# Gated recurrence of one layer: decayed keys and queries carried from level to level, gate units cut in quarters

## The reference, cut to what matters

```
f = lb + (1 - lb) * sigmoid(f_logit)
log_f = log(max(f, 1e-6)); key = 1 - f
state = 0
for t: state = exp(log_f[t])[:, None] * state + key[t][:, None] * v[t][None, :]
       out[t] = q[t] @ state
```

## Time and profile before

| | |
|---|---|
| median of 3 runs | 3363.87 us (3363.17 to 3366.28) |
| the profiled execution | 3358.75 us |
| its span | 3356.6 us |
| TensorE busy | 3220.8 us, 96% |
| VectorE busy | 1618.3 us, 48% |
| ScalarE busy | 1085.7 us, 32% |
| GpSimd busy | 322.1 us, 10% |
| granted TensorE clock, mean | 0.98 |

### The profile page before, as it was taken

One profiled execution on the slowest core, in us unless ns is written; L12 is line 12 of the kernel. 1 busy time (PEld: TensorE's weight loads), 2 busy tenths in 40 slices (PEclk: granted clock), 3 DMA queues, 4 the chain that ended last, 5 costly groups with the idle time before them and its releaser, 6 DMA issues.

```text
span 3356.6 us, 38850 instructions
## 1 busy us (share of the span) xinstructions
PE 3220.8 (96%) x15546; PEld 2652.5 (79%) x15546; DVE 1618.3 (48%) x1917; ACT 1085.7 (32%) x1157; POOL 322.1 (10%) x178
## 2 busy tenths in 40 slices
PE   6986899999999899999999999999999999999999
PEld 5865698888888789888888777888888777888887
DVE  5365454555334644555534755444433674454433
ACT  2223233444322333444423332233322332233232
POOL 1003110011000001001100200101100120011000
PEclk9998899999999999999999999999999999999999
DMA  3410131222332123122233212222232212222223
GB/s 138 127 46 30 38 144 45 88 99 88 113 126 76 51 74 128 38 98 90 100 112 91 81 63 88 88 101 93 95 106 103 77 63 88 88 88 100 100 100 113
DMA packets 47578, 299.94 MB, mean 89 GB/s; under 512 B 7075, under 2 KB 7331, under 8 KB 13012
## 3 DMA queue, kind: packets, MB, share of 16 engines
q1 hardware_dynamic: 42336, 288.01, 24.3%
q10 hardware_dynamic: 5108, 10.02, 1.3%
HBM read 293.26 MB, written 4.75 MB: 89 GB/s over the span
## 4 chain that ended last, share of the span: by engine, by line
PE 90%; DVE 5%; ACT 2%; issue 1%; POOL 1%; DMA 0%; another core or an unknown queue 0%; ACTq 0%; DVEq 0%; SPq 0%; POOLq 0%
PE G L409 80%; PE psS L869 1%; PE G L876 1%; PE psS L681 1%; DVE wL L1342 1%; PE psT L901 1%; PE psT L490 1%; ACT wH L982 1%; PE psS L465 1%; PE psS L768 1%; PE G L775 1%; DVE mxt L1532 1%; PE psS L462 0%; DMA x<-in_x 0%; DVE ws L1814 0%
## 5 line engine op out<-in xcount | busy, mean ns | idle before, releaser
L409 PE MATMUL G<-hH,wH 128*128 128x512 f32 x2624 | 1042.3, 397 | 11.0 <-DVE wL L1342 5.9
L409 PE MATMUL G<-hH,wL 128*128 128x512 f32 x2624 | 1027.5, 392 | 2.1 <-issue 2.1
L409 PE MATMUL G<-hL,wH 128*128 128x512 f32 x2624 | 1027.7, 392 | 0.0
L1342 DVE TENSOR_TENSOR wL<-raw,wH 128x2048 fp32r<-128x2048 f32 x266 | 647.7, 2435 | 673.3 <-ACT wH L982 673.0
L409 PE MATMUL G<-wsr,wH 128*128 128x512 f32 (+1 forms) x2400 | 713.9, 381 | 14.3 <-DVE ws L2031 9.7
L982 ACT ACTIVATE wH<-raw 128x2048 fp32r<-128x2048 f32 x266 | 506.8, 1905 | 456.0 <-PE G L409 441.5
L409 PEld LDWEIGHTS G<-hH,wH 128*128 128x128 f32 x2624 | 497.6, 190 | 121.0 <-issue 16.4
L409 PEld LDWEIGHTS G<-hH,wL 128*128 128x128 f32 x2624 | 496.3, 189 | 108.3 <-issue 2.5
L409 PEld LDWEIGHTS G<-hL,wH 128*128 128x128 f32 x2624 | 496.7, 189 | 103.4 <-issue 2.4
L409 PEld LDWEIGHTS G<-wsr,wH 128*128 128x128 f32 x2400 | 445.4, 190 | 101.3 <-DVE ws L2031 10.6
L409 PE MATMUL G<-wsr,wL 128*128 128x512 f32 (+1 forms) x1200 | 456.2, 380 | 0.0
(11 more groups left out here) (259 smaller groups left out, 2769.6 us busy)
## 6 DMA issues: line engine op xcount, KB each, us to landing
raw<-in_units SPq DMA_DIRECT2D x266, 1024.0 KB, 4.8
ws<-bias_rows SPq DMA_DIRECT2D x2, 1536.0 KB, 14.8
bias_rows<-ws ACTq DMA_DIRECT2D x1, 2560.0 KB
x<-in_x SPq DMA_DIRECT2D x4, 512.0 KB, 8.2
ws<-in_mem ACTq DMA_DIRECT2D x2, 1024.0 KB, 4.9
ws<-bias_rows ACTq DMA_DIRECT2D x1, 2048.0 KB, 8.4
out_x<-x SPq DMA_DIRECT2D x4, 512.0 KB, 7.6
ws<-in_decay ACTq DMA_DIRECT2D x1, 1280.0 KB, 13.0
```

Of the source, the lines that this page charges most:

```text
L409: mm = pe.matmul(o, mv if swap else wt, wt if swap else mv, start=first and n == 0, stop=last and n == 2)
L1342: V.tensor_tensor(wL[:, g.p, :], raw[:, g.p, :], wH[:, g.p, :].bitcast(F32), ALU.subtract)\
```

## The change

The running sum now starts anew in every block of 4 tokens (HG_BLOCK). ACT takes exp(cum) and exp(-cum) once, per head, and the exponential of each block's last sum, the decay of the whole block. DVE multiplies by q and key for level 0, and multiplies the key by its block's decay. POOL forms the decays of blocks of 8, 16, 32, 64 and 128 tokens by five small products of pairs, 128x256, 128x128, 128x64, 128x32 and 128x16 (`level_sums`, now line 2155). From level to level, DVE then multiplies in place (`grow`): keys of even blocks by the decay of the odd neighbour, queries of odd blocks by that of the even one, per head and behind that head's scores. `hz_ready` now counts heads. The banks of levels 6 and 7 are read by ACT (`hc_ready`). The two gate units are cut into quarters of 12 matmuls, one behind each level, unit one behind levels 0 to 3, unit two behind levels 4 to 7. The two steps that follow the gate units stand, on DVE, behind level 5 and behind level 6's products.

```
-HG_CHUNK = 64
+HG_BLOCK = 4
...
+        sums = {4: ws[:, RST, :].rearrange("p (h n) -> p h n", h=4)}
+        at = 0
+        for half in (8, 16, 32, 64, 128):
+            n = S // half
+            sums[half] = ws[:, SD + 2, at:at + 4 * n].rearrange("p (h n) -> p h n", h=4)
+            at += 4 * n
@@ -660,17 +667,18 @@
                     for lev in range(8):
-                        pe.wait_ge(hz_ready, lev + 1)
-                        zk = ZA if lev % 2 == 0 else ZB
-                        zq = ZB if lev == 0 else zk
                         for h in range(4):
                             n = lev * 4 + h
-
-                            wait(pe, hm_ready, n - 1)
-                            if lev == 0:
+                            pe.wait_ge(hz_ready, n + 1)
+
+                            if n >= 26:
+                                pe.wait_ge(hc_ready, n - 25)
+                            else:
+                                wait(pe, hm_ready, n - 1)
+                            if n == 0:
 
                                 pe.wait_ge(ms_ready, c.stat.v)
-                            k_, q_ = ws[:, zk + h, :], ws[:, zq + h, :]
+                            k_, q_ = ws[:, (ZB if lev == 0 else KEY) + h, :], ws[:, ZA + h, :]
                             if lev < 6:
                                 parts = [(ct * P, ct * P, ct * P, P) for ct in range(4)]
                             elif lev == 6:
@@ -682,9 +690,19 @@
                                                start=True, stop=True)
                             mm.then_inc(hs_done, 1)
 
-                        if lev in (1, 3):
-                            plain(h_op)
-                    pe.wait_ge(hm_ready, 32)
+                        q = lev % 4
+                        if q == 0:
+                            take_unit()
+                            take_job()
+                        for k in (2 * q, 2 * q + 1):
+                            for t in range(2):
+                                w0 = k * 256 + t * P
+                                mm = passes(G[:, c.job.p * 2 + t, :], w0, w0 + P, h_op, k, slice(0, S), k == 0, k == KT - 1)
+                        if q == 3:
+                            end_job(mm)
+                            c.unit.off += 1
+                    pe.wait_ge(hm_ready, 24)
+                    pe.wait_ge(hc_ready, 8)
@@ -1158,23 +1176,24 @@
-                    for lev in range(8):
-                        z = flat(ZA if lev % 2 == 0 else ZB, 4)
-                        act.wait_ge(he_in, lev + 1)
-                        if lev == 0:
-                            activation(flat(ZA, 4), flat(ZB, 4), ACT.Exp, scale=-1.0)
-                            activation(flat(ZB, 4), flat(ZB, 4), ACT.Exp).then_inc(he_exp, 1)
-                            step()
-                        elif 2 ** (lev + 1) < HG_CHUNK:
-                            activation(z, z, ACT.Exp).then_inc(he_exp, 1)
+                    act.wait_ge(scan_ready, 1)
+                    activation(ws[:, RST, :], flat(CUM, 4).rearrange("p (n l) -> p n l", l=4)[:, :, 3], ACT.Exp)\
+                        .then_inc(t4_ready, 1)
+                    act.wait_ge(tn_ready, c.nrm.v + 4)
+                    for h in range(4):
+                        activation(ws[:, ZA + h, :], ws[:, CUM + h, :], ACT.Exp)
+                        activation(ws[:, ZB + h, :], ws[:, CUM + h, :], ACT.Exp, scale=-1.0).then_inc(he_exp, 1)
+                    step()
+                    step(store(ws[:, GG:GG + 2, :], ACT.Silu))
+                    for n in range(24, 32):
+                        act.wait_ge(hs_done, n + 1)
+                        b, h = psS[:, n % 2, :], n % 4
+                        if n < 28:
+                            ins = activation(hsx1[:, h], b.rearrange("p (k q) -> p k q", q=P)[:, 0:2, :], ACT.Copy)
                         else:
-
-                            half = 2 ** (lev + 1)
-                            z0, z1 = blocks(z, half)
-                            activation(z0, z0, ACT.Exp)
-                            activation(z1, blocks(flat(CUM, 4), half)[1], ACT.Exp).then_inc(he_exp, 1)
-                        if lev in (3, 5):
-                            step(store(ws[:, GG + lev - 3:GG + lev - 1, :], ACT.Silu))
+                            ins = activation(ws[:, SX2 + h, :], b, ACT.Copy)
+                        ins.then_inc(hc_ready, 1)
+                    step(store(ws[:, GG + 2:GG + 4, :], ACT.Silu))
@@ -1735,45 +1754,55 @@
-                    gq, key = flat(GQ, 4), flat(KEY, 4)
-
-                    def mask(lev):
+
+                    for h in range(4):
+                        dve.wait_ge(he_exp, h + 1)
+                        V.tensor_tensor(ws[:, ZA + h, :], ws[:, ZA + h, :], ws[:, GQ + h, :], ALU.mult)
+                        V.tensor_tensor(ws[:, ZB + h, :], ws[:, ZB + h, :], ws[:, KEY + h, :], ALU.mult)\
+                            .then_inc(hz_ready, 1)
+                    dve.wait_ge(t4_ready, 1)
+                    for h in range(4):
+
+                        dve.wait_ge(hz_ready, h + 1)
+                        V.tensor_tensor(ws[:, KEY + h, :].rearrange("p (n l) -> p n l", l=4),
+                                        ws[:, ZB + h, :].rearrange("p (n l) -> p n l", l=4),
+                                        sums[4][:, h, :].unsqueeze(2).to_broadcast([P, S // 4, 4]), ALU.mult)\
+                            .then_inc(hz_ready, 1)
+                    step(inputs(1))
+
+                    def grow(h, half):
+
+                        k0, q1 = blocks(ws[:, KEY + h, :], half)[0], blocks(ws[:, ZA + h, :], half)[1]
+                        pair = sums[half][:, h, :].rearrange("p (n two) -> p n two", two=2)
+                        f0, f1 = pair[:, :, 0:1], pair[:, :, 1:2]
+                        n = S // (2 * half)
+                        if half == 128:
+                            k0, q1, f0, f1, n = k0[:, 0:1, :], q1[:, 1:2, :], f0[:, 1:2, :], f1[:, 0:1, :], 1
+                        V.tensor_tensor(k0, k0, f1.to_broadcast([P, n, half]), ALU.mult)
+                        V.tensor_tensor(q1, q1, f0.to_broadcast([P, n, half]), ALU.mult).then_inc(hz_ready, 1)
+
+                    for lev in range(7):
                         for h in range(4):
                             n = lev * 4 + h
                             dve.wait_ge(hs_done, n + 1)
-                            b = psS[:, n % 2, :].rearrange("p (k q) -> p k q", q=P)
-                            d = ws[:, DD + h, :].rearrange("p (k q) -> p k q", q=P)
-                            if lev == 0:
-                                ins = V.tensor_tensor(d, b, hmask[:, 0:1, :].to_broadcast([P, 4, P]), ALU.mult)
-                            elif lev < 6:
-                                ins = V.copy_predicated(d, hmask[:, lev:lev + 1, :].bitcast(I32).to_broadcast([P, 4, P]), b)
-                            elif lev == 6:
-                                ins = V.tensor_copy(hsx1[:, h], b[:, 0:2, :])
-                            else:
-                                ins = V.tensor_copy(ws[:, SX2 + h, :], psS[:, n % 2, :])
-                            ins.then_inc(hm_ready, 1)
-
-                    for lev in range(8):
-                        if lev == 1:
-                            mask(0)
-                        half = 2 ** (lev + 1)
-                        z = flat(ZA if lev % 2 == 0 else ZB, 4)
-                        if lev >= 2:
-                            mask(lev - 1)
-                        if lev in (3, 5):
+                            if lev > 0:
+                                if h == 0 and lev > 1:
+                                    dve.wait_ge(tb_ready, lev - 1)
+                                dve.wait_ge(hz_ready, n + 1)
+                                grow(h, 2 ** (lev + 1))
+                            if lev < 6:
+                                b = psS[:, n % 2, :].rearrange("p (k q) -> p k q", q=P)
+                                d = ws[:, DD + h, :].rearrange("p (k q) -> p k q", q=P)
+                                if lev == 0:
+                                    ins = V.tensor_tensor(d, b, hmask[:, 0:1, :].to_broadcast([P, 4, P]), ALU.mult)
+                                else:
+                                    wait(dve, hm_ready, n - 3)
+                                    ins = V.copy_predicated(d, hmask[:, lev:lev + 1, :].bitcast(I32)
+                                                            .to_broadcast([P, 4, P]), b)
+                                ins.then_inc(hm_ready, 1)
+                        if lev == 5:
                             step(None, act_too=True)
-                        dve.wait_ge(he_exp, lev + 1)
-                        if lev == 0:
-                            V.tensor_tensor(flat(ZA, 4), flat(ZA, 4), key, ALU.mult)
-                            ins = V.tensor_tensor(flat(ZB, 4), flat(ZB, 4), gq, ALU.mult)
-                        else:
-                            z0, z1 = blocks(z, half)
```

(41 more changed lines are left out.)

7 lines of the change are left out of this document (4 added, 3 removed).

## The result

The changed kernel takes **3309.33 us** (median of 4 runs, 3307.80 to 3310.54); the kernel before took 3363.52 beside it (4 runs, 3358.33 to 3366.28). The ratio is 0.984, its 95% interval 0.9823 to 0.9857.

The account below looks back on a forecast made before the run. TensorE, waiting between levels of gate-stage scores and slowed by the clock, was taken as the bound. Level 0 ending at 256.1, plus 38.8 and 11.2, put value products at 306.1 against 345.24: 39.1 us less, 3325; range 3316 to 3336.

Parts of the forecast that it names:

- Levels 1 to 5: Gate stage: head waits set by two score-bank halves, then a quarter unit; 7.76 us a level, 38.8 in all, bounds 6.67 to 8.2.
- Levels 6 and 7: Gate stage's last levels, banks read by ScalarE: scores, a 0.4 copy wait and a quarter each; together 11.2 us.
- Level 0: Gate stage's first level and its quarter: from 243.14 to 256.1 us, masks coming when they came before.
- Of which some 1.0 falls on the split: Level 0: of 1.8 us for GpSimd's five small products, some 1.0 lengthens VectorE's first split.
- VectorE is what is late: Level 0: VectorE's products, second input copy and split end at 248.1, so TensorE's 2.1 us of lead is worth nothing.
- heads 2 and 3 run at the low clock as before (3.78): Level 0 on TensorE: idle from about 245.2, then these heads take 3.78 us, from 249.1 to 252.9.
- Beyond it everything keeps its shape: Behind the gate stage: remaining work ends some 9.5 us after value products start, before the norm asks for GpSimd at 13.7.
- I take the 39.1 from the median: Whole program: the stage's 39.1 us gain subtracted from the runs' median, 3363.87, not the profiled execution's 3358.75; gives 3325.
- better than forecast: Rival: quarters cover all waits (6.67 a level, 5.5 us less), no clock fall at level 0 (3.5 less); 3316, chance 0.08.
- The tail on the norm: Rival: hH copies, tails and a split behind the last quarter delay the norm by up to 8.1 us; 3333, chance 0.08.
- the clock: Rival: waits near 1 us drop TensorE's clock; half the stage so, 3343, chance 0.07; all of it, 3362, 0.02.
- VectorE as the bound: Rival: VectorE's small products with a repeated operand run stretched in the levels; 3376 at the longest stretch, chance 0.04.

Follow-up runs that it names:

- copy_first: The changed kernel with each head's copy out of the score bank ahead of its two products in levels 1 to 5; 3310.65 us.
- double_grow: The changed kernel with each head's two products of levels 1 to 5 made twice, the second pair into an unread tile; 3328.01 us.
- four_banks: The changed kernel with scores alternating over four banks (both halves of two tiles) instead of two; 3300.87 us.
- before_again: The kernel before, unchanged, profiled and timed once more; 3357.97 us.
- old_quarters: The kernel before with its gate units cut in quarters behind every level, following steps moved accordingly, old chain between levels kept; 3336.01 us.
- before_padded: The kernel before with 64 tiny one-column matmuls ahead of everything on TensorE, moving its later code; 3366.90 us.
- warm_waits: The kernel before with extra unused matmuls filling most of TensorE's waits behind levels 0, 2, 4, 5 and 6; 3346.81 us.

## Why the prediction was right and wrong

- **The mechanism was right.** The level's chain over GpSimd, ScalarE and VectorE is gone, the masks of a head are what TensorE waits for, the two-half bank sets the period, and the clock is at 1.00 from the end of the first quarter on. copy_first and double_grow moved the period to within 0.1 us of what the same arithmetic gave (7.0 and 9.0), and four_banks took it to TensorE's floor.
- **Levels 1 to 5**: 38.2 for 38.8. The wait ahead of head 3 was mis-sized (0.16 for 0.42). I had taken 1.4 a head on VectorE; the starts are 1.29 apart when nothing interrupts (0.34 + 0.34 + 0.61). The bound of 8.2 a level took 1.57 a head, the three durations added up (0.42 + 0.42 + 0.73); no run shows such a head.
- **Levels 6 and 7**: 11.27 for 11.2 (the terms as written add up to 11.1).
- **Level 0**, 13.0 forecast (243.14 to 256.1), 11.5 measured. Three steps failed. "Of which some 1.0 falls on the split" was wrong: nothing fell on it. "VectorE is what is late" left out the path over ScalarE: VectorE was through with its products and the second copy at 243.70, and the split waited for the rounding until 243.81. The masks came 4.3 us after the stage's start (246.04 - 241.78) and not 5.0 (248.1 - 243.14). And "heads 2 and 3 run at the low clock as before (3.78)" was wrong: the clock was still at 1.00 when they began and fell only after 248, so they took 2.52. The quarter then got more of the low clock than forecast, 3.86 us and not 3.2.
- **"Beyond it everything keeps its shape"** failed as a statement on one execution: 1.4 us came ahead of the stage and 7.0 in the second model's last layer, 2.07 of them the stall and about 5 three falls of the granted clock. Five profiles of unchanged code behind the stage (before, after, each again, copy_first) span 2930.6 to 2939.0 us there. That the falls and the stall were in the one execution and not in the other was luck, and it made the gain look larger.
- **"I take the 39.1 from the median"** is the step that cost most. The median of three runs, 3363.87, stood 5.1 above its own profiled execution and 7 above the median of the 39 later runs. From 3356.6 the forecast would have been 3317.5: above 3309.3 and 3311.6 by 8.2 and 5.9. What is left then is 2.1 in the stage, 1.4 ahead of it, and 2.4 to 4.7 behind it.
- **The rivals.** The first, "better than forecast" at 3316 with 0.08, was the nearest, but not by its mechanism: a level of 6.67 without waits needed the four banks (6.31 then). The tail on the norm, the clock and VectorE as the bound did not come. The 0.04 on VectorE's repeated operand is answered by the rows: it costs what a plain one does.
- **The range** took in only the unknowns of the stage and 1.5 us for the runs; the kernel's own scatter (3350.9 to 3368.0 over 51 runs of the kernel before) is ten times that.

**What stays open.** A stall of 1.5 to 2.1 us stands in the second model's last layer in four profiles, all of programs with the old order of levels (before, before_again, old_quarters, before_padded), and in none of the ten others, warm_waits with the old order among them. What causes it no run here shows. Executions of the same code behind the stage spread by 9 us. In the last layer the traces put that down to the stall and to falls of the granted clock; why the clock falls there in some executions and not in others, with TensorE as busy in both, is not shown.

## What to carry to other kernels

Price a chain over several engines by the waits that it leaves on the bound engine and by the clock behind each wait; then ask what is next, as the two-half bank was here (10.7 us for one more pair of halves, more than all of the reordering). Cover in small pieces behind every wait is worth more than the same cover in one lump, since a lump longer than the wait is idle cover: 20.5 us here without touching the chain. And before subtracting a sum worked out to a tenth, look at how far the few runs lie from their own profiled execution: here that one choice was 5.1 of the 15.7 us by which the forecast missed, and 7.3 against the later runs.

## What was not expected of the hardware

- GpSimd took 4.68 us for five products of 256 down to 16 elements, 0.9 each; the line through its 1024 and 2048 elements (0.2 us fixed) had given 1.8.
- VectorE's split of 128x2048 beside these kept its 2.28 us, while beside one subtraction of 2048 elements on GpSimd it had taken 4.78. The 4.78 are what it would take if it waited until GpSimd was done (234.29 to 236.91) and then ran its own 2.2, an estimate from these rows.
- A float32 matmul of one column took 0.43 us in a row of 64 at the program's start. By its pace that is half clock, though the profile's clock reads 1.00 there: the passes behind it start 0.43 apart, as they do at 0.50 in the changed kernel's first quarter. At 1.00 the norm's sums take 0.23 each (8 in 1.84 us), as much as a matmul of 128 columns in a head (0.895 / 4).
- TensorE busy 76% and 75% of a stretch had a granted clock of 0.81 in one and 1.00 in the other (double_grow). The busy share alone does not tell it. In the kernel before the clock fell twice to 0.50 for a short time while TensorE was busy without a pause (2643, 2670).
